# Loading and computing the opening of a hybrid layer by halves of the features

## The chip, the core and the metric

One core of a Trainium2 chip runs the whole layer in one launch. The metric is the device time of the launch in microseconds; lower is better. Five engines work side by side and meet only at semaphores: TensorE (PE, matmuls), VectorE (DVE), ScalarE (ACT), GpSimd (POOL) and SyncE (SP, which issues most of the DMAs). ScalarE and GpSimd issue DMAs too, in the order of their own instructions.

## The reference, cut to what matters

384 tokens (128 of context, 256 latent) of 1024 features go through a layer. At its start stand the modulation (a silu of a conditioning vector times `w_ada`, 12 chunks of 512 columns here: shift is chunks 0 and 1, scale chunks 2 and 3) and the first projection `w_in`:

```python
mod = (silu(c) @ w_ada + b_ada).reshape(1, N_MOD, D_MODEL)       # one for the context, one for the latents
h = rmsnorm(x, g_pre_mix) * (1.0 + scale_a) + shift_a
z = h @ w_in            # u, q, k, v, o (512 columns each) and 16 gate columns
y = concat(pool_mixer(u), bidirectional_mlstm(q, k, v, o, gates)) @ w_out
x = x + gate_a * rmsnorm(y, g_post_mix)
x = x + gate_f * rmsnorm(moe(rmsnorm(x, g_pre_ffn) * (1 + scale_f) + shift_f), g_post_ffn)
```

`moe` routes each token to 6 of 64 experts (1024 to 2 x 256 to 1024). Chunks 0 and 2 of `w_ada` are the first 512 features of shift and scale, chunks 1 and 3 the last 512. In z the features are summed over, so the first 512 features of h and of `w_in`'s rows give half of every sum.

## The kernel before, in words

**Weights.** The 20 weight chunks of 2 MB of the opening (a0 to a11 of `w_ada`, q, k, v, o, u of `w_in`, w0 and w1 of `w_out`, s) go through four slots `w_gu`, chunk number i of the list `order` (L444) in slot i mod 4. SyncE issues their loads in order (L629 to 641; o before a7), q in two halves of four feature blocks (L635 with semaphore `q_in`, L636). Before a chunk that reuses a slot it waits until the slot's last chunk was used (`gu_used`).

**Modulation.** `ada(i)` (L1685) multiplies a chunk of `w_ada` into bank 6 or 7 on TensorE for i under 4; `ada_evac` (L1055) adds the bias into `modrow`, `one_plus` (L1068) makes (1 + scale) times the gain, four small matmuls (L1728) turn the rows into columns in bank 6, and a copy (L1078) puts them into `modT`. For i from 4 to 9 VectorE makes the products itself (`ada_sums`, L1101, L1125 and L1130), in banks 4 and 5 for a4, 6 and 7 for the others.

**Tokens.** The normalised tokens are transposed into banks 0 to 5 (L1723). `shifted` applies scale and shift to a block of 128 features, blocks 0 to 3 on VectorE (L1083) and 4 to 7 on ScalarE (L748). Products are made with an fp32 operand split in two parts: `high` (L731, L740) and `high_tokens` (L751, L756) on ScalarE make the rounded parts `w_hi` and `tT_hi`, `low` (L518, L524) on GpSimd and `low_tokens` (L1086, L1089) on VectorE the rests `w_lo` and `tT_lo`. `PARTS` lists the feature blocks that one `high_tokens` takes. Each product is three matmuls (`three`, L529 to 531).

**Products.** `z_chunk` (L1733) runs over the two halves of the features of q, k, v, o, u, and in a half over the four (or three) units of the chunk, each in a bank of its own (`z_bank`). q comes first, then the gates' products in bank 0, then k, which waits until VectorE is done with a4 (banks 4 and 5). There are two buffers `w_hi`; the next chunk's half waits until the half before last is used.

**ScalarE's order.** After the last `high_tokens` ScalarE issues seven DMAs (L769 to 777: `poolm`, `w_pool`, state_C, `pool_scale`, state_n, the router's weights and bias), and only then comes `high(2)`, the first half of k. Rows of 4 bytes: `pool_scale` has 512 of them, state_n 1024; `w_pool` and state_C have 512 + 1024 rows of 512 bytes.

Of the kernel before, what the change touches and what calls it, by code (L numbers as in the profile page):

```python
# [14 lines left out]
P = 128  # L15
D = 1024
NC = D // P
T_CTX, T_LAT = 128, 256
T = T_CTX + T_LAT
# [84 lines left out]
ALU = mybir.AluOpType  # L104
# [70 lines left out]
def build_layer(nc, t_in, t_out):  # L175
    with ExitStack() as ctx:
# [254 lines left out]
        def row_from_dram(engine, dst, m, first, semaphore):  # L431
# [11 lines left out]
        COL = {"u": 0, "q": MW, "k": 2 * MW, "v": 3 * MW, "o": 4 * MW}  # L443
        order = ["a0", "a1", "a2", "a3", "q", "a4", "a5", "k", "v", "a6", "a7", "o", "u", "a8", "a9",  # L444
                 "w0", "w1", "a10", "a11", "s"]
# [48 lines left out]
        def z_bank(n):  # L494

            w, i = z_units[n]
            return (1, 2, 6, 7)[i] if w == "q" else 2 + i

# [7 lines left out]

        PARTS = ((0, 2), (2, 4), (4, 8))

# [115 lines left out]
        def _(sp):  # L624
            for i in range(NT):
                src = t_in["x_prompt"][0] if i == 0 else t_in["x_sample"][0, P * (i - 1):P * i, :]
                sp.dma_start(x[:, i, :], src).then_inc(x_in, 16)
            a7, o = chunk["a7"], chunk["o"]
            for name in order[:a7] + ["o", "a7"] + order[o + 1:]:  # L629
                i = chunk[name]  # L630
                s = i % PSLOTS
                if i >= PSLOTS:
                    sp.wait_ge(gu_used[s], i // PSLOTS)
                if name == "q":
                    sp.dma_start(w_gu[s][:, 0:NC // 2, :], chunk_source(name)[:, 0:NC // 2, :]).then_inc(q_in, 16)  # L635
# [81 lines left out]
        def _(a):  # L717
# [33 lines left out]
            def high_tokens(first, end):  # L751
                if first < 4:
                    a.wait_ge(h1_dve, 2 * end)
                else:
                    a.wait_ge(h1_act, NC)
                a.activation(tT_hi[first // 4][:, first % 4:end - 4 * (first // 4), :], hT[:, first:end, :], ACT.Copy)\  # L756
                    .then_inc(th_ready, 1)

            a.wait_ge(modT_ready, 1)
            shifted(4)  # L760
            shifted(5)
            high_tokens(*PARTS[0])
            shifted(6)
            high_tokens(*PARTS[1])
            high(1)
            shifted(7)
            high_tokens(*PARTS[2])

            a.dma_start(poolm[:, :, :].rearrange("p g n -> p (g n)"), t_in["pool_constants"]).then_inc(pool_in, 16)  # L769
# [38 lines left out]
            a.wait_ge(mod_a_ready, 1)  # L808
            for m in range(2):
# [224 lines left out]
        def _(v):  # L1034
# [38 lines left out]
            for i in (0, 2, 1, 3):  # L1073
                ada_evac(i)
            v.wait_ge(mod_ready, 4)
            one_plus(2, 0).then_inc(mod_a_ready, 1)
            v.wait_ge(modT_done, 1)
            v.tensor_copy(modT[:, :, :, :].rearrange("p a c m -> p (a c m)"), bank(6, P, P + 32)).then_inc(modT_ready, 1)  # L1078
            v.wait_ge(modT_ready, 1)

            def shifted(c):
                for m, (lo, hi) in enumerate(((0, T_CTX), (T_CTX, T))):
                    v.tensor_scalar(hT[:, c, lo:hi], psum[:, T * c + lo:T * c + hi], modT[:, 1, c, m:m + 1],  # L1083
                                    modT[:, 0, c, m:m + 1], ALU.mult, ALU.add).then_inc(h1_dve, 1)
# [7 lines left out]

            shifted(0)
            shifted(1)
            shifted(2)
            low_tokens(0)
            shifted(3)
            low_tokens(1)
            low_tokens(2)

            def ada_sums(i, c_first=0, c_end=NC):  # L1101

                n = chunk[f"a{i}"]
                s = n % PSLOTS
                done = 15 * sorted(ada_acc).index(i)
                if c_first == 0:
                    v.wait_ge(gu_in[s], 16 * (n // PSLOTS + 1))
                    if i >= 6:
                        wait_chunk(v, f"a{i - 1}")
                    if i == 4:  # L1110
                        v.wait_ge(h1_act, NC)
# [29 lines left out]
            ada_sums(4)  # L1141
            ada_sums(5, 0, 3)

            v.wait_ge(gates_done, 1)
            for b, dst in enumerate((g_in, g_lf)):
                own.add(v.tensor_scalar(dst[0:32, :], bank(0, 0, T)[64 * b:64 * b + 32, :], b_gate[0:32, b:b + 1], None, ALU.add))
                for tile in range(NT):
                    ins = v.tensor_scalar(dst[32:36, P * tile:P * tile + P],
                                          bank(0, 0, T)[64 * b + 32:64 * b + 36, natural(1, tile)],
                                          b_gate[32:36, b:b + 1], None, ALU.add)  # L1150
                    own.add(ins)
# [15 lines left out]
            v.tensor_tensor(g_b[:, :], g_b[:, :], g_mx[:, :], ALU.add).then_inc(scans_ready, 1)  # L1167
            ada_sums(5, 3)
            v.wait_ge(scans_ready, 1)
# [463 lines left out]
        def _(g):  # L1633
# [18 lines left out]

            for k in range(12):
                low(g, k)
# [29 lines left out]
        def _(t):  # L1684
# [32 lines left out]
            ada(0)  # L1717
            ada(1)
            t.wait_ge(const_in, 16)
# [4 lines left out]
            ada(2)  # L1724
            ada(3)
            t.wait_ge(mod_a_ready, 1)
            for i in range(4):
                ins = t.matmul(bank(6, P + 8 * i, P + 8 * i + 8), modrow[:, i, :],  # L1728
                               ident.rearrange("p (j r) -> p j r", j=4)[:, :, 0:2], start=True, stop=True)
            ins.then_inc(modT_done, 1)  # L1730


            def z_chunk(w):  # L1733
# [3 lines left out]
                for half in range(2):  # L1737
                    t.wait_ge(w_lo_ready, SPLIT.index((w, half)) + 1)
                    if w == "q":
                        t.wait_ge(tl_ready, 1 if half == 0 else len(PARTS))  # L1740
                    for n in units:
                        i = z_units[n][1]
                        prior = before(n)
                        if half == 0 and prior is not None:
# [4 lines left out]
                        for j in range(4):  # L1749
                            c = 4 * half + j  # L1750
                            if n == 0 and c == PARTS[1][0]:
                                t.wait_ge(tl_ready, 2)
                            if w in "qk":
# [12 lines left out]
            for w in "qkvou":  # L1766
# [454 lines left out]
```

## Time and profile before

| | us |
|---|---|
| three runs | 761.12, 762.65, 764.17 |
| median | 762.65 |
| the profiled execution | 762.65 |
| its span in the trace | 760.6 |
| TensorE busy | 700.4 (92%) |
| VectorE busy | 404.3 (53%) |
| ScalarE busy | 190.5 (25%) |
| GpSimd busy | 84.7 (11%) |
| HBM read | 254.64 MB, 340 GB/s over the span |

The span runs from the first to the last instruction of the trace; 2.05 us lie around it. The layer's stages in the trace: the opening up to 42 us, the projections up to about 141 us, the mixers and `w_out` up to about 209 us, then the router and the experts, whose weight loads start at 214.5 us. Busy time is a sum over stages with different limits, so each step is read from the rows of its own stage. Durations in the rows are those of one execution.

### The profile page before, as it was taken

The page shows a single profiled execution, that of the slowest core. Times are in us where ns is not written, and L with a number is a line of the kernel's source. Part 1 is how long each engine was busy: PE and PEld are TensorE (multiplying, and loading weights), DVE is VectorE, ACT ScalarE, POOL GpSimd, SP SyncE. Part 2 cuts the span into 40 slices and gives each one's busy share as a digit, 9 for nine tenths or more (in the row PEclk, how much of TensorE's full clock was granted, in tenths as well). Part 3 has the DMA queues.
Part 4 walks back from the last instruction along what each step waited for, and adds up shares of the span by engine and source line. Part 5 has one row for each costly group of instructions (what it writes and reads, how often), then busy time and mean ns, then how long its engine had stood idle before and what let it go on. Part 6 is the DMA issues. An engine that isn't in the chain of part 4 may idle for free.

```text
span 760.6 us, 11595 instructions
## 1 busy us (share of the span) xinstructions
PE 700.4 (92%) x4241; PEld 403.9 (53%) x4241; DVE 404.3 (53%) x1004; ACT 190.5 (25%) x320; POOL 84.7 (11%) x49
## 2 busy tenths in 40 slices
PE   1679999899989999999999999999999999989785
PEld 1579888688866645544444444444444445433232
DVE  3078999477085754454544545454454464434234
ACT  3145422474264112212111111211211111111003
POOL 2244444411400100000000000000000000000000
PEclk9879999999999999999999999999999999999999
DMA  9998576623669559879999999999999999999982
GB/s 325 382 379 260 181 258 225 248 86 94 211 247 422 245 209 399 332 320 382 421 419 421 423 421 419 421 420 420 420 420 421 420 421 421 421 422 418 421 343 92
DMA packets 56766, 259.17 MB, mean 341 GB/s; under 512 B 7296, under 2 KB 9952, under 8 KB 31488
## 3 DMA queue, kind: packets, MB, share of 16 engines
q1 hardware_dynamic: 48720, 249.05, 81.5%
q0 software_dynamic: 1808, 5.92, 2.3%
q10 hardware_dynamic: 6176, 3.40, 1.5%
q8 instruction: 36, 0.59, 0.3%
q14 instruction: 26, 0.21, 0.1%
HBM read 254.64 MB, written 3.71 MB: 340 GB/s over the span
## 4 chain that ended last, share of the span: by engine, by line
PE 65%; DMA 14%; DVE 12%; SPq 5%; ACT 2%; issue 1%; ACTq 0%; DVEq 0%
PE psum L2056 19%; DMA w_gu<-in_w_expert_gu 11%; PE psum L2068 10%; PE psum L1949 9%; PE psum L2027 7%; PE psum L529 4%; PE psum L531 4%; PE psum L530 4%; DVE psum L1130 3%; DMA w_gu<-in_w_ada 3%; PE psum L1930 3%; DVE f_acc L1537 2%; SPq L665 2%; SPq L674 2%; PE psum L1961 1%
## 5 line engine op out<-in xcount | busy, mean ns | idle before, releaser
L2056 PE MATMUL psum<-w_gu,hgT 128*32 128x512 f32 (+1 forms) x1280 | 192.1, 594 | 10.3 <-DMA w_gu<-in_w_expert_gu 10.3
L2056 PEld LDWEIGHTS psum<-w_gu,hgT 128*32 128x32 f32 (+1 forms) x1280 | 58.1, 119 | 136.6 <-issue 136.4
L1537 DVE TENSOR_TENSOR f_acc<-f_acc,psum 128x512 f32<-128x512 f32 x156 | 106.1, 687 | 45.5 <-PE psum L2027 42.3
L2068 PE MATMUL psum<-w_dn,actT 128*32 128x512 f32 (+1 forms) x640 | 98.5, 596 | 0.5 <-ACT actT L951 0.5
L1522 DVE SCALAR_TENSOR_TENSOR act<-sil,wsl,psum 128x256 f32<-128x256 f32 x27 | 18.3, 680 | 135.4 <-ACT sil L976 127.1
L2027 PE MATMUL psum<-y_hi,onehotT 128*128 128x512 f32 x156 | 67.7, 434 | 4.5 <-DVE f_acc L1537 2.5
L524 POOL TENSOR_TENSOR w_lo<-w_gu,w_hi 128x2048 fp32r<-128x2048 f32 x14 | 64.3, 4599 | 62.9 <-ACT w_hi L740 62.9
L1949 PE MATMUL psum<-onehot,h_hi 128*128 128x512 f32 (+1 forms) x168 | 67.3, 401 | 0.0
L1949 PE MATMUL psum<-onehot,h_lo 128*128 128x512 f32 (+1 forms) x168 | 64.9, 386 | 0.0
L1528 DVE TENSOR_TENSOR y_lo<-psum,y_hi 128x1024 fp32r<-128x1024 f32 x27 | 33.0, 1224 | 54.2 <-ACT y_hi L980 54.2
L2027 PE MATMUL psum<-y_lo,onehotT 128*128 128x512 f32 x156 | 61.3, 393 | 0.0
L980 ACT ACTIVATE y_hi<-psum 128x1024 fp32r<-128x1024 f32 x27 | 27.6, 1024 | 122.0 <-PE psum L2068 122.0
L2068 PEld LDWEIGHTS psum<-w_dn,actT 128*32 128x32 f32 (+1 forms) x640 | 27.0, 119 | 57.6 <-issue 56.8
L976 ACT ACTIVATE sil<-psum 128x256 f32<-128x256 f32 x27 | 10.4, 384 | 183.6 <-PE psum L2056 183.6
L432 POOL DMA_DIRECT2D gate_ctx<-mod_rows x1 | 0.6, 586 | 483.0 <-DVE act L1522 483.0
L971 ACT ACTIVATE hgT<-psum 128x512 f32<-128x512 f32 (+1 forms) x56 | 32.6, 582 | 80.9 <-PE psum L1949 80.9
L1130 DVE SCALAR_TENSOR_TENSOR psum<-w_gu,scT,psum 128x512 f32<-128x512 f32 x72 | 48.2, 750 | 0.0
L529 PE MATMUL psum<-w_hi,tT_hi 128*128 128x512 f32 x120 | 47.3, 394 | 0.0
L531 PE MATMUL psum<-w_hi,tT_lo 128*128 128x512 f32 x120 | 46.7, 390 | 0.0
L530 PE MATMUL psum<-w_lo,tT_hi 128*128 128x512 f32 x120 | 46.7, 389 | 0.0
L740 ACT ACTIVATE w_hi<-w_gu 128x2048 fp32r<-128x2048 f32 x14 | 26.8, 1914 | 72.1 <-PE psum L531 28.2
L1949 PEld LDWEIGHTS psum<-onehot,h_hi 128*128 128x128 f32 x168 | 31.5, 187 | 23.5 <-issue 18.1
(293 smaller groups left out, 864.0 us busy)
## 6 DMA issues: line engine op xcount, KB each, us to landing
w_gu<-in_w_expert_gu SPq DMA_DIRECT2D x128, 1024.0 KB, 19.8
w_dn<-in_w_expert_down SPq DMA_DIRECT2D x64, 1024.0 KB, 18.8
w_gu<-in_w_ada SPq DMA_DIRECT2D x12, 2048.0 KB, 15.9
w_gu<-in_w_in SPq DMA_DIRECT2D x4, 2048.0 KB, 8.7
w_gu<-in_w_out SPq DMA_DIRECT2D x2, 2048.0 KB, 10.4
bc<-mod_rows POOLq DMA_DIRECT2D x6, 512.0 KB, 7.3
w_gu<-in_w_in SPq DMA_DIRECT2D x2, 1024.0 KB, 15.8
w_gu<-in_w_shared_gu SPq DMA_DIRECT2D x1, 2048.0 KB, 9.3
```

The costliest lines, as they stand in the source:

```text
L524: engine.tensor_tensor(w_lo[s][:, cs, :], w_gu[s][:, cs, :], w_hi[half][:, :, :].bitcast(F32), ALU.subtract)\
L529: t.matmul(out, lhs[0], rhs[0], start=start, stop=False)
L530: t.matmul(out, lhs[0], rhs[1], start=False, stop=False)
L531: return t.matmul(out, lhs[1], rhs[0], start=False, stop=stop)
L971: a.activation(dst, src, ACT.Copy).then_inc(hgT_ready, 1)
L1130: ins = v.scalar_tensor_tensor(out, w, k, part, ALU.mult, ALU.add)
L1528: v.tensor_tensor(y_lo[:, :], bank(3, 0, 1024), y_hi[:, :].bitcast(F32), ALU.subtract).then_inc(y_ready, 1)
L1537: v.tensor_tensor(dst, dst, bank(5 + n), ALU.add).then_inc(f_added, 1)
L1949: ins = t.matmul(bank(c % 2, 0, width), part[:, i, c, :], onehot[b % 2][:, i, 0:width], start=(n == 0), stop=(n == 2 * NT - 1))
L2027: ins = t.matmul(bank(5 + n), onehotT[par][:, i, :], part[:, 512 * n:512 * (n + 1)], start=(part is y_hi), stop=(part is y_lo))
L2056: ins = t.matmul(bank(2)[rows, :], column(c)[:, rows], w_gu[s][:, c, :], start=(c == 0), stop=(c == NC - 1), tile_position=(0, rows.start))
L2068: ins = t.matmul(bank(3 + n)[rows, :], actT[:, j, rows], w_dn[s][:, j, 512 * n:512 * (n + 1)], start=(j == 0), stop=(j == 1), tile_positio ...
```

## The change

The opening is done in two halves of the features. SyncE loads a0, a2 and the first half of q, then a1, a3, the second half of q, a4, k, v, and a5 only behind v. The modulation is made per half (`modulation(half)`, `modulation_T(half)`), so that `mod_a_ready` and `modT_ready` count to 2. Blocks 3 and 7 are shifted on ScalarE, the other six on VectorE; `PARTS` has four entries of two blocks. On TensorE the transposes stand in front of ada(2), ada(1) behind the first half's modulation, ada(3) in front of q's third unit and the second half's modulation in front of q's fourth. q's third unit is in bank 0, the gates' products in bank 6, and a5's sums are no longer begun before the gates' evacuation. GpSimd makes the first `w_lo` before it issues its small loads.

```diff
-        order = ["a0", "a1", "a2", "a3", "q", "a4", "a5", "k", "v", "a6", "a7", "o", "u", "a8", "a9",
+        order = ["a0", "a2", "q", "a1", "a3", "a4", "a5", "k", "v", "a6", "a7", "o", "u", "a8", "a9",
...
-            return (1, 2, 6, 7)[i] if w == "q" else 2 + i
+            return (1, 2, 0, 7)[i] if w == "q" else 2 + i
...
-        PARTS = ((0, 2), (2, 4), (4, 8))
+        PARTS = ((0, 2), (2, 4), (4, 6), (6, 8))
+        ON_ACT = (3, 7)
...
-            for name in order[:a7] + ["o", "a7"] + order[o + 1:]:
+            issued = ["a0", "a2", "q", "a1", "a3", "q", "a4", "k", "v", "a5", "a6", "o", "a7"] + order[chunk["u"]:]
+            for turn, name in enumerate(issued):
...
             a.wait_ge(modT_ready, 1)
-            shifted(4)
-            shifted(5)
+            shifted(3)
             high_tokens(*PARTS[0])
-            shifted(6)
             high_tokens(*PARTS[1])
             high(1)
+            a.wait_ge(modT_ready, 2)
             shifted(7)
             high_tokens(*PARTS[2])
+            high_tokens(*PARTS[3])
...
+            def modulation(half):
+
+                ada_evac(half)
+                ada_evac(2 + half)
+                v.wait_ge(mod_ready, 2 * half + 2)
+                v.scalar_tensor_tensor(modrow[:, 2 + half, :], modrow[:, 2 + half, :], 1.0, grow[:, 0, half, :],
+                                       ALU.add, ALU.mult).then_inc(mod_a_ready, 1)
+                v.wait_ge(modT_done, half + 1)
+                v.tensor_copy(modT[:, :, 4 * half:4 * half + 4, :],
...
-            shifted(0)
-            shifted(1)
-            shifted(2)
-            low_tokens(0)
-            shifted(3)
-            low_tokens(1)
-            low_tokens(2)
+            for half in range(2):
+                modulation(half)
+                for c in range(4 * half, 4 * half + 3):
+                    shifted(c)
+                low_tokens(2 * half)
+                low_tokens(2 * half + 1)
...
             ada_sums(4)
-            ada_sums(5, 0, 3)
...
-            ada_sums(5, 3)
+            ada_sums(5)
...
+            low(g, 0)
             g.wait_ge(gu_in[3], 16)
             g.dma_start(wgs[:, :, :], w_in[:, :, 5 * MW:5 * MW + 16]).then_inc(gate_in, 16)
...
             ada(0)
-            ada(1)
...
             ada(2)
-            ada(3)
...
+            modulation_T(0)
+            ada(1)
...
+                        if (w, half, i) == ("q", 0, 2):
+                            ada(3)
+                        if (w, half, i) == ("q", 0, 3):
+                            modulation_T(1)
...
-                        ins = three(t, bank(0, 0, T), (wg_hi[:, c, :], wg_lo[:, c, :]),
+                        ins = three(t, bank(6, 0, T), (wg_hi[:, c, :], wg_lo[:, c, :]),
```

## Rows read from the trace of the kernel before

**Rows 1.** Busy time in one stretch; columns: us, five engines, clock, DMA share, GB/s.
```profile
300.00:700.00 400.00, 392.90 (x2338) 181.09 (x2336) 191.75 (x503) 67.55 (x114) 0.00 (x0) 1.00 0.99 409
```

**Rows 2.** Chain of waits in order of time; columns: start, us, what.
```profile
10.80 21.52 DMA w_gu<-in_w_ada
```

**Rows 3.** Timeline of the opening; columns: start, us, engine, line, operation, idle before, releaser.
```profile
15.35 3.64 PE L1697 MATMUL psum<-w_gu,scT 128*32 128x128 f32 x64 [15.35 <-DMA w_gu<-in_w_ada]
...
23.82 2.84 PE L1723 MATMUL psum<-const,xn 128*128 128x128 f32 x24
...
26.95 1.95 PE L1697 MATMUL psum<-w_gu,scT 128*32 128x128 f32 x64 [0.29 <-DMA w_gu<-in_w_ada]
...
32.37 2.57 PE L1697 MATMUL psum<-w_gu,scT 128*32 128x128 f32 x64 [3.46 <-DMA w_gu<-in_w_ada]
...
35.02 1.91 ACT L740 ACTIVATE w_hi<-w_gu 128x2048 fp32r<-128x2048 f32 x1 [22.28 <-DMA w_gu<-in_w_in]
...
35.50 0.42 DVE L1070 SCALAR_TENSOR_TENSOR modrow<-modrow,grow 128x256 f32<-128x256 f32 x1
...
35.98 1.88 PE L1728 MATMUL psum<-const,modrow 128*128 128x8 f32 x8 [1.05 <-DVE modrow L1070]
37.01 4.50 POOL L524 TENSOR_TENSOR w_lo<-w_gu,w_hi 128x2048 fp32r<-128x2048 f32 x1 [1.15 <-ACT w_hi L740]
...
38.12 2.40 DVE L1083 TENSOR_SCALAR hT<-psum,modT 128x128 f32<-128x128 f32 x6
...
40.66 1.67 DVE L1089 TENSOR_TENSOR tT_lo<-hT,tT_hi 128x768 fp32r<-128x768 f32 x1
...
42.48 0.66 PE L529 MATMUL psum<-tT_hi,w_hi 128*128 128x384 f32 x1 [4.62 <-DVE tT_lo L1089]
```

**Rows 4.** Timeline from the gates' products to u, one engine after the other.
```profile
61.75 0.34 PE L529 MATMUL psum<-tT_hi,wg_hi 128*128 128x384 f32 x1
...
66.68 0.41 PE L529 MATMUL psum<-tT_hi,w_hi 128*128 128x384 f32 x1 [0.52 <-issue]
...
64.01 1.40 DVE L1125 TENSOR_SCALAR psum<-w_gu,scT 128x512 f32<-128x512 f32 x2
...
101.46 0.69 DVE L1179 COPY v<-psum 128x512 f32<-128x512 f32 x1 [0.34 <-PE psum L531]
...
138.30 1.91 ACT L740 ACTIVATE w_hi<-w_gu 128x2048 fp32r<-128x2048 f32 x1 [3.50 <-PE psum L531]
```

**Rows 5.** ScalarE's queue in the timeline; then DMA issues: KB each, us to landing.
```profile
48.03 6.29 ACTq L773 DMA_DIRECT2D small<-in_pool_scale  x1
...
55.80 3.54 ACTq L776 DMA_DIRECT2D w_router<-in_w_router  x1
...
59.93 1.92 ACT L740 ACTIVATE w_hi<-w_gu 128x2048 fp32r<-128x2048 f32 x1 [11.83 <-issue]
...
c0n<-in_state_C ACTq DMA_DIRECT2D x1, 512.0 KB, 11.9
...
w_gu<-in_w_in SPq DMA_DIRECT2D x1, 2048.0 KB, 23.9
```

**Rows 6.** Timeline: a VectorE instruction beside one of GpSimd.
```profile
77.39 4.78 DVE L1165 TENSOR_SCALAR g_lf<-g_mx 36x384 f32<-36x384 f32 x1
...
77.33 4.62 POOL L524 TENSOR_TENSOR w_lo<-w_gu,w_hi 128x2048 fp32r<-128x2048 f32 x1 [6.20 <-ACT w_hi L740]
```

**Rows 7.** DMA queues at 53 to 54, then 54 to 55: packets, MB, share.
```profile
q10 hardware_dynamic: 32, 0.33, 78.8%
q1 hardware_dynamic: 32, 0.07, 16.9%
...
q1 hardware_dynamic: 146, 0.30, 78.5%
q10 hardware_dynamic: 133, 0.06, 21.2%
```

**Rows 8.** Busy time and clock, the columns of rows 1.
```profile
46.00:47.00 1.00, 1.00 (x5) 1.00 (x4) 0.00 (x0) 0.97 (x3) 1.00 (x1) 0.50 1.06 391
```

More of the change, by code:

```diff
@@ L627, in _ @@
                 sp.dma_start(x[:, i, :], src).then_inc(x_in, 16)
-            a7, o = chunk["a7"], chunk["o"]
-            for name in order[:a7] + ["o", "a7"] + order[o + 1:]:
+            issued = ["a0", "a2", "q", "a1", "a3", "q", "a4", "k", "v", "a5", "a6", "o", "a7"] + order[chunk["u"]:]
+            for turn, name in enumerate(issued):
                 i = chunk[name]
@@ L633, in _ @@
                     sp.wait_ge(gu_used[s], i // PSLOTS)
+                if name == "q" and "q" in issued[turn + 1:]:
+                    sp.dma_start(w_gu[s][:, 0:NC // 2, :], chunk_source(name)[:, 0:NC // 2, :]).then_inc(q_in, 16)
+                    continue
                 if name == "q":
-                    sp.dma_start(w_gu[s][:, 0:NC // 2, :], chunk_source(name)[:, 0:NC // 2, :]).then_inc(q_in, 16)
                     sp.dma_start(w_gu[s][:, NC // 2:NC, :], chunk_source(name)[:, NC // 2:NC, :]).then_inc(gu_in[s], 16)
@@ L751, in high_tokens @@
             def high_tokens(first, end):
[L752 to L755, printed above, removed]
+                here = [c for c in range(end) if c in ON_ACT]
+                a.wait_ge(h1_dve, 2 * (end - len(here)))
+                if here:
+                    a.wait_ge(h1_act, 2 * len(here))
                 a.activation(tT_hi[first // 4][:, first % 4:end - 4 * (first // 4), :], hT[:, first:end, :], ACT.Copy)\
@@ L807, in _ @@
                             g_b[32 * d:32 * d + H, T_CTX - 1:T_CTX]).then_inc(m_out, 16)
-            a.wait_ge(mod_a_ready, 1)
+            a.wait_ge(mod_a_ready, 2)
             for m in range(2):
@@ L1071, in one_plus @@
                                               ALU.add, ALU.mult)
[L1073 to L1079, printed above, removed]
+            def modulation(half):
[6 more added lines that the diff above has]
+                v.tensor_copy(modT[:, :, 4 * half:4 * half + 4, :],
+                              bank(6, P, P + 32).rearrange("p (a c m) -> p a c m", a=2, c=NC)[:, :, 4 * half:4 * half + 4, :])\
+                    .then_inc(modT_ready, 1)
+                v.wait_ge(modT_ready, half + 1)
             def shifted(c):
+                if c + 1 in ON_ACT:
+                    v.wait_ge(h1_act, 2 * ON_ACT.index(c + 1) + 2)
                 for m, (lo, hi) in enumerate(((0, T_CTX), (T_CTX, T))):
@@ L1110, in ada_sums @@
                     if i == 4:
-                        v.wait_ge(h1_act, NC)
+                        v.wait_ge(h1_act, 2 * len(ON_ACT))
                     elif i == 5:
@@ L1141, in _ @@
             ada_sums(4)
-            ada_sums(5, 0, 3)
             v.wait_ge(gates_done, 1)
             for b, dst in enumerate((g_in, g_lf)):
-                own.add(v.tensor_scalar(dst[0:32, :], bank(0, 0, T)[64 * b:64 * b + 32, :], b_gate[0:32, b:b + 1], None, ALU.add))
+                own.add(v.tensor_scalar(dst[0:32, :], bank(6, 0, T)[64 * b:64 * b + 32, :], b_gate[0:32, b:b + 1], None, ALU.add))
                 for tile in range(NT):
                     ins = v.tensor_scalar(dst[32:36, P * tile:P * tile + P],
-                                          bank(0, 0, T)[64 * b + 32:64 * b + 36, natural(1, tile)],
+                                          bank(6, 0, T)[64 * b + 32:64 * b + 36, natural(1, tile)],
                                           b_gate[32:36, b:b + 1], None, ALU.add)
@@ L1650, in _ @@
                         .then_inc(gate_in, 16)
-            for k in range(12):
+            for k in range(1, 12):
                 low(g, k)
@@ L1724, in _, with modulation_T @@
             ada(2)
-            ada(3)
[L1726 to L1730, printed above, removed]
+            def modulation_T(half):
+                t.wait_ge(mod_a_ready, half + 1)
+                if half:
+                    t.wait_ge(modT_ready, half)
+                for i in (half, 2 + half):
+                    ins = t.matmul(bank(6, P + 8 * i, P + 8 * i + 8), modrow[:, i, :],
+                                   ident.rearrange("p (j r) -> p j r", j=4)[:, :, 0:2], start=True, stop=True)
+                ins.then_inc(modT_done, 1)
+            modulation_T(0)
+            ada(1)
             def z_chunk(w):
@@ L1739, in z_chunk @@
                     if w == "q":
-                        t.wait_ge(tl_ready, 1 if half == 0 else len(PARTS))
+                        t.wait_ge(tl_ready, 2 * half + 1)
                     for n in units:
                         i = z_units[n][1]
+                        if (w, half, i) == ("q", 0, 2):
+                            ada(3)
+                        if (w, half, i) == ("q", 0, 3):
+                            modulation_T(1)
                         prior = before(n)
@@ L1750, in z_chunk @@
                             c = 4 * half + j
-                            if n == 0 and c == PARTS[1][0]:
-                                t.wait_ge(tl_ready, 2)
+                            if n == 0 and j == 2:
+                                t.wait_ge(tl_ready, 2 * half + 2)
                             if w in "qk":
```

## The prediction, made before the changed kernel was run

> **What bounds the kernel now.** I read four views, in this order. First the page and the windows. From 300 us on the DMA engines are busy 0.99 of the time at 409 GB/s and TensorE 392.9 of 400 us [rows 1]: the expert stage is full on both, its loads start only when the slots of the opening come free, so what the opening gains or loses moves the end by as much. Second the chain of waits of the opening: loads of `w_gu` up to 32.37, then a serial stretch (ada(3), the transposes of the modulation, shift and scale, tokens' parts) until the first product of q at 42.48 [rows 2, 3]. Third TensorE: q's products 42.48 to 61.75, the gates' to about 66.2, k's from 66.68, and from there its only idle time of note is 0.7 us until u is done at 138.3, where `high(11)`, which waits for it, starts [rows 3, 4]. VectorE runs beside it: v's last copy at 101.46 waited 0.34 us for TensorE, and from there VectorE is full up to `u_tok` at 141.36 [rows 4]. So TensorE and VectorE meet at 101.46 with 0.34 us between them, and a shift of TensorE's chain from k on is a shift of the end. Fourth, what lets k start: not q. ScalarE issues seven DMAs from 46.62 to 59.83, can make `w_hi` of k only at 59.93 (k landed at 34.97 + 23.9 = 58.9), GpSimd needs 4.6 us more for `w_lo`, and k starts at 66.68, 0.5 us after the gates' products [rows 5]. **The start of k is set twice over**, by TensorE's own work (66.2) and by ScalarE's queue (66.6). A change of the first alone gives nothing.
>
> **The loads.** Bytes on SP's queue up to a load fix its landing, as the engines are full: 3.67 MB at 15.35, 7.87 at 26.95, 9.97 at 32.37, 11.0 (first half of q) at 35.02 [rows 3]. By these points the new order lands a0 at 15.35, a2 about 21, half of q 23.8, a1 29.6, a3 35.0, the rest of q 37.7 to 38.3 (GpSimd's small loads dip the rate), a4 43, k 48.5. The bytes ahead of k's end shrink by one chunk; v takes the place of a5, which now waits until q is used.
>
> **First half.** TensorE: ada(0) 15.35 to 18.99, transposes (2.84, up to 5 at half rate) to 22.3, ada(2) 1.95 to 24.3; evacuations 0.49, `one_plus` half of 0.42, four small matmuls half of 1.88, copy 0.19 [rows 3]: modT's first half at 26.2 instead of 38.08. VectorE's six shifts 2.40 to 28.65, parts of the tokens about 0.85 each. `w_hi` 23.8 to 25.7 and `w_lo` to 30.3; the first `low_tokens` has two SBUF inputs, and one such row ended 0.8 us after GpSimd's w_lo did (42.33 against 41.51) [rows 3], so 31.2 and 32.1. ada(1) at 29.6 takes 2.5 to 3.6 us: 32.1 to 33.3. Then q's first two units, 24 matmuls; warm ones start 0.175 us apart (from 61.58, with the gates' first at 61.75 [rows 4]), 4.2 us: 37.2. **q starts about 9.7 us earlier** (32.8 against 42.48).
>
> **Second half.** ada(3) 37.2 to 39.2; evacuation 39.8; `one_plus` 0.3; unit 2 of q 39.2 to 41.3; modulation_T(1) 41.8; copy 42.1; shifts to 44.5; `low_tokens` 45.5 and 46.4; unit 3 runs beside them. q's second half, 48 matmuls x 0.174 = 8.3, to 54; gates 4.4 (61.75 to 66.15), to 58.4. That is 7.8 us before 66.2. Moved work: a4's sums run 46.4 + 1.3 (casts) + 10.7 (they ended at 64.01, where a5's start) = 58.4 [rows 4], in time for k, which waits for them. The first three channels of a5's sums (4.0 us: 1.40 + 2.6, 64.01 to 67.94 [rows 4]) now lie behind the gates, in VectorE's way; in exchange VectorE starts 5.5 us earlier, and L1165, which stood 4.4 us behind GpSimd (4.78 for 384 columns, GpSimd's w_lo ran 77.33 to 81.95 [rows 6]), falls elsewhere. VectorE reaches a5's end near 88 against 89.57: it is not the bound, and is priced at nothing; if its cover went it would cost up to 4 us. The bank changes (q's unit 2, the gates) cost nothing: bank 0 is free after the shifts, bank 6 after the copy of modT. GpSimd's five small issues (some 3 us) now follow its first `w_lo`, 30.3 to 33.6, and land some 6 us later, before the casts at 46.4. The new waits: VectorE's third shift of a half waits for ScalarE's two (0.86 us, side by side); TensorE's modulation_T(1) stands in front of q's unit 3 alone, and that unit is back before `low_tokens` of the second half is ready, so its wait is covered; without that cover it would cost 0.8 us.
>
> **ScalarE's queue: where the gain goes.** Its seven issues stand behind the last `high_tokens`, which starts at 44.6 instead of 46.62. Their 13.2 us are waiting, not issuing: L773 took 6.29 and ended at 54.32, as `poolm`'s last packets went [rows 7], L776 took 3.54 and ended at 59.34, as state_C landed (47.47 + 11.9) [rows 5]. How fast they drain depends on what SP's queue has in flight. While `poolm` moved, SP's queue (q1) and ScalarE's (q10) got 32 packets each in one us; in the next, 146 of q1 (0.30 MB) stood against 133 of q10 (0.06 MB), 78.5% of the time against 21.2% [rows 7]: **one packet in turn, 2 KB against 0.5 KB**. Before, q1 ran dry behind k, since v waited until q was used (61.75). After, `poolm` moves 48.5 to 52.5; q1 then holds about 41 packets per engine of k and v (behind `poolm` about 19 were left before; the start is 1.9 us earlier, at the 12 per us of 0.39 MB), and **a5 adds 64 from 55.2**, a6 64 from 59.5, since a4 is done sooner. w_pool and state_C have (512 + 1024)/16 = 96 packets per engine, a pair costs 0.785 x 16/146 + 0.212 x 16/133 = 0.086 + 0.026 = 0.112 us. The unknown is how much of it must be gone before L776 ends. Lower bound 56 packets (state_n's 64 and w_router's 8 per engine then find the room that was left when L773 ended): 52.9 + 56 x 0.112 + the slowest engine's 0.8 = 60.0, and one more us for the issues: free at 61.2, k at 61.2 + 1.92 + 4.6 + 0.1 = 67.8. Upper bound for these two: all 96, free at 63.8, k at 70.5. I take 69.0, +2.3 against 66.68; the row nearest to it (L776 ended with state_C's landing) is for the later end. Below nothing: were the 13.2 us a fixed length, k would start 1.9 to 2.1 earlier.
>
> **The clock.** TensorE would stand idle from 58.4 to 69. After 4.6 us of idling at 37.9 its granted clock read 0.50 (1.2 GHz) until 47.1, 0.50 still at 46 to 47 [rows 8]: 4.6 us at half rate, 2.3 lost. Taken: 2.1; bounds 0 (short gap) and 2.3.
>
> **Sum.** The profiled execution took 762.65 with a span of 760.6, and 762.65 is also the median of the three runs. +2.3 (start of k) + 2.1 (clock) + 0 (VectorE) = +4.4: **767.0**, slower by 0.6%.
>
> **A rule against a row.** The `one_plus` of the second half starts at 39.8, and GpSimd's `w_lo` of q's second half at 39.7 to 40.3. Beside GpSimd the rows show waiting of TENSOR_TENSOR [rows 3] and TENSOR_SCALAR [rows 6], none of SCALAR_TENSOR_TENSOR with both inputs in SBUF. The Trainium skill (SBUF — State Buffer, Who interferes with whom) says that a VectorE instruction with two SBUF inputs contends with a GpSimd one that reads SBUF, and that the one issued first blocks the other; by it `one_plus` would wait too. No row here shows that form. If it waits, it waits out GpSimd's 4.5 us.
>
> **Rivals.**
> Not slower: `one_plus` comes second and waits to 44.3. Then shifts end at 47.8, q ends at 57.4 to 59, gates at 61.6 to 63.6, ScalarE issues from 47.9. `poolm` is through at 55.8, q1 has about 3 packets per engine left and a5 comes only at 58.5 or later, when the 96 small ones are nearly gone: 3 x 0.112 + 93 x 0.027 = 2.9 us, 58.7 to 60.3. k starts at 66.5 to 67.5, after a gap of 3 to 5 us (clock 0 to 2): +0 to +3, 764. It decides from a `one_plus` that starts after GpSimd. For it: the two are 0.5 us apart. Against: in the new order the landing that starts GpSimd is the one that slips. Chance 0.27.
> Worse: L776 needs state_n's 4-byte packets gone too, 96 more per engine, each in turn with a 2 KB packet of a5 and a6: 0.099 x 60 to 80 = 6 to 8 us more, k at 76: +9.5 + 2.1, 774. For: in the quarter microseconds to 59.3 most of them had gone. Against: L774 itself took only 1.42. Chance 0.17.
> Faster: the seven issues keep their length, or q10 is not held by a5; k at 64.6, gap 6 us: -2.1 + 0 to 2, about 761.5; were k free to start at the gates' end, 58.9 for 66.7, 754.9. For: VectorE, TensorE and k's landing (about 50) would all allow it. Against: ScalarE's 11.83 us before `high` [rows 5]. Chance 0.20, most of it on gains above 4 us that some looser queue would bring.
> That the change does not do what it says (q not earlier): only if ada(1) or the first shift were late by 10 us; under 0.02, within the others.
>
> **How the numbers follow.** Forecast 0.36 (765.5 to 769), not slower 0.27 (762 to 766), worse 0.17 (771 to 776), faster 0.20 (754 to 762). The range for 8 in 10: 757 to 774. About 0.5% (3.8 us) is what a measurement of this kernel can tell from no change. Slower by more: 0.27 of the forecast + 0.17 + 0.03 = 0.47; within: 0.09 + 0.22 + 0.06 = 0.37; faster: 0.14 + 0.02 = 0.16.
>
> **What would show it.** First product of q at 32 to 34; `one_plus` of the second half short (0.3) or over 4 us; q's end at 54 or 57 to 59; ScalarE's issues from 44.6 or 47.9 and their length (13.2, 17, 25 us); a gap of TensorE before k and the granted clock behind it; q1 and q10 with equal packets at 55 to 62; every later stage shifted by k's amount. The prediction is wrong if ScalarE's `high` of k starts before 58, or if the chain from k on is no longer rigid.

## The result and the profile after

| | us | ratio to before, 95% interval |
|---|---|---|
| kernel before, 15 runs | 762.63 (761.12 to 764.4) | |
| changed kernel, 15 runs beside them | 765.4 (763.6 to 767.46) | 1.0034 [1.0022, 1.0047] |
| changed kernel again, 8 runs, beside 19 of before (762.46) | 766.51 (764.17 to 768.02) | 1.005 [1.0033, 1.0068] |
| the profiled executions: before, after | 762.65, 765.4 (spans 760.6, 763.3) | |

The change makes the kernel slower by 0.3 to 0.5%. The forecast was 767.0 with a range of 757 to 774. On the first set the whole interval lies inside 0.5%, a case that had been given 0.37 against 0.47 for slower by more; the second set straddles that bound. Further down each ratio is to runs of the kernel before on the same chip (their medians: 761.76, 762.46 and 762.2), so the ratios can be compared with each other, the times only roughly.

The opening did what it was meant to do. The timeline of the changed kernel, opening (start, us, engine, line, operation, idle time before and its releaser); it answers to [rows 3]:

```profile
15.42 3.40 PE L1706 MATMUL psum<-w_gu,scT 128*32 128x128 f32 x64 [15.42 <-DMA w_gu<-in_w_ada]
...
23.43 1.91 ACT L743 ACTIVATE w_hi<-w_gu 128x2048 fp32r<-128x2048 f32 x1 [10.66 <-DMA w_gu<-in_w_in]
...
25.43 4.52 POOL L525 TENSOR_TENSOR w_lo<-w_gu,w_hi 128x2048 fp32r<-128x2048 f32 x1 [16.56 <-ACT w_hi L743]
...
27.89 3.74 DVE L1099 TENSOR_TENSOR tT_lo<-hT,tT_hi 128x768 fp32r<-128x768 f32 x2
29.23 3.33 PE L1706 MATMUL psum<-w_gu,scT 128*32 128x128 f32 x64 [4.13 <-DMA w_gu<-in_w_ada]
...
32.49 0.45 PE L530 MATMUL psum<-tT_hi,w_hi 128*128 128x384 f32 x1
...
39.40 0.29 DVE L1081 SCALAR_TENSOR_TENSOR modrow<-modrow,grow 128x128 f32<-128x128 f32 x1
...
40.34 4.57 POOL L525 TENSOR_TENSOR w_lo<-w_gu,w_hi 128x2048 fp32r<-128x2048 f32 x1 [7.18 <-ACT w_hi L743]
...
45.87 0.66 PE L530 MATMUL psum<-tT_hi,w_hi 128*128 128x384 f32 x1 [2.20 <-DVE tT_lo L1099]
```

q's first product starts at 32.49, ten microseconds before the 42.48 of [rows 3]. Its second half starts at 45.87, after 2.20 us of idling.

The same timeline from there to k and v, and at the first expert load; it answers to [rows 4, 5]:

```profile
44.15 0.33 ACTq L772 DMA_DIRECT2D poolm<-in_pool_constants  x1
...
45.56 7.77 ACTq L776 DMA_DIRECT2D small<-in_pool_scale  x1
...
53.36 2.42 ACTq L777 DMA_DIRECT2D c0n<-in_state_n  x1
55.80 3.58 ACTq L779 DMA_DIRECT2D w_router<-in_w_router  x1
59.41 0.50 ACTq L780 DMA_DIRECT2D b_router<-in_b_router  x1
60.01 1.91 ACT L743 ACTIVATE w_hi<-w_gu 128x2048 fp32r<-128x2048 f32 x1 [15.03 <-issue]
...
62.00 9.35 POOL L525 TENSOR_TENSOR w_lo<-w_gu,w_hi 128x2048 fp32r<-128x2048 f32 x2 [17.10 <-ACT w_hi L743]
63.33 3.58 DVE L1161 SCALAR_TENSOR_TENSOR g_t<-g_lf 36x384 f32<-36x384 f32 x1
...
66.61 0.66 PE L530 MATMUL psum<-tT_hi,w_hi 128*128 128x384 f32 x1 [6.42 <-POOL w_lo L525]
...
102.82 0.69 DVE L1187 COPY v<-psum 128x512 f32<-128x512 f32 x1 [0.35 <-PE psum L532]
...
217.38 2.77 SPq L655 DMA_DIRECT2D w_gu<-in_w_expert_gu  x2
```

The gates' products end at 60.2 instead of 66.2. ScalarE makes `w_hi` of k at 60.01, as before (59.93, [rows 5]): its issues began 2.5 us earlier (44.15 for 46.62) and were held 2.6 us longer (15.8 us for 13.2). k starts at 66.61, as before (66.68, [rows 4]), and TensorE has idled for 6.42 us. The six microseconds won at the gates are all lost in front of k.

Then k costs more. Busy time and clock of the changed kernel in four stretches (us, five engines, clock, DMA share, GB/s), and of the kernel before in the last two of them:

```profile
45.00:49.00 4.00, 3.13 (x10) 3.16 (x11) 3.86 (x12) 0.00 (x0) 0.00 (x0) 0.59 1.10 418
62.00:70.00 8.00, 3.39 (x12) 3.42 (x13) 7.93 (x6) 6.85 (x9) 8.00 (x2) 0.57 1.05 383
142.00:147.00 5.00, 4.14 (x24) 3.32 (x28) 0.91 (x3) 1.62 (x4) 4.18 (x1) 1.00 1.04 398
158.00:166.00 8.00, 8.00 (x38) 7.32 (x37) 4.64 (x18) 4.42 (x16) 0.00 (x0) 0.57 0.01 3
```

```profile
142.00:147.00 5.00, 5.00 (x18) 3.81 (x16) 0.00 (x0) 1.56 (x3) 2.81 (x1) 0.66 1.05 396
158.00:166.00 8.00, 8.00 (x61) 7.13 (x61) 7.11 (x25) 5.62 (x22) 0.00 (x0) 1.00 0.00 0
```

TensorE's granted clock is at half (1.2 GHz) for part of q's second half and again around the start of k. So v's last copy comes 36.21 us behind k's start instead of 34.78: 102.82 against 101.46, +1.36. From there to the first expert load 114.56 us pass for 113.03. In this stretch before has one low spell of about 3 us, at 143 to 146, and after one of about 7 us, at 158 to 165; +1.53. From the load to the end of the span it is 545.92 against 546.11, -0.19. The sum, +2.70, is the difference of the spans. So only +1.36 lies in the stretch that the change touches. The +1.53 comes with the length and the place of a low spell; the second execution of the changed kernel, below, has a shorter spell there and no such loss.

### The profile page after: what moved, and what is told of

It is laid out like the page before. It is cut to its first block, busy times and chain, and to the rows that moved or that the text cites. A ratio compares the mean times of both kernels' runs of the same rounds, so it can differ in the third digit from the quotient of the medians.

```text
span 763.3 us, 11603 instructions
## 1 busy us (share of the span) xinstructions
PE 702.9 (92%) x4241; PEld 405.9 (53%) x4241; DVE 410.7 (54%) x1011; ACT 189.4 (25%) x317; POOL 84.8 (11%) x49
## 4 chain that ended last, share of the span: by engine, by line
PE 64%; DMA 13%; DVE 11%; SPq 5%; ACT 2%; ACTq 2%; issue 1%; POOL 1%; DVEq 0%
PE psum L2074 19%; DMA w_gu<-in_w_expert_gu 11%; PE psum L2086 10%; PE psum L1967 9%; PE psum L2045 7%; DVE psum L1139 3%; PE psum L530 3%; PE psum L532 3%; PE psum L531 3%; PE psum L1948 3%; DMA w_gu<-in_w_ada 2%; DVE f_acc L1545 2%; SPq L668 2%; SPq L677 2%; PE psum L1979 1%
```

## The experiments

### Is it ScalarE's queue that holds k?

The four issues that wait longest are moved behind v's parts, in the changed kernel and, to see what they are worth alone, in the kernel before.

```diff
@@ ScalarE, behind the last high_tokens
             a.dma_start(poolm, ...); a.dma_start(w_pool, ...); a.dma_start(c0n, state_C ...)
-            a.dma_start(pool_scale, ...)
-            a.dma_start(c0n, state_n ...)
-            a.dma_start(w_router, ...)
-            a.dma_start(b_router, ...)
@@ ScalarE, behind high(5), in front of the g_post_ffn issues
+            (the same four)
```

> The changed kernel with ScalarE's last four issues (pool_scale, state_n, the router's two) moved from in front of high(2) to behind high(5); the three large ones stay. Theory (ScalarE's queue holds k): high(2) starts as soon as k has landed and q's first half is used, about 50 to 53 us instead of 60.0; w_lo of k is ready before 60; k starts at 60.2, straight behind the gates' products, instead of 66.61, and its granted clock stays 1.00. Time 765.4 - 6.4 - 1.4 = 757.6, up to 760 if one of VectorE's scans falls behind GpSimd's w_lo. Rival (k held by its landing, or by VectorE's a4 sums at 58.6): k starts at 60 to 63. Rival (VectorE's chain is the bound after all): k starts at 60.2, but v's last copy moves by under 3 us and the time is 763 or more.

Measured: **755.3 us**, ratio 0.9921 [0.9894, 0.9948]. Timeline of this kernel:

```profile
49.16 1.92 ACT L743 ACTIVATE w_hi<-w_gu 128x2048 fp32r<-128x2048 f32 x1 [3.36 <-DMA w_gu<-in_w_in]
...
57.28 1.59 DVE L1139 SCALAR_TENSOR_TENSOR ada_acc<-w_gu,scT,psum 128x512 f32<-128x512 f32 x2
...
58.93 0.44 PE L530 MATMUL psum<-tT_hi,w_hi 128*128 128x384 f32 x1
...
93.78 0.69 DVE L1187 COPY v<-psum 128x512 f32<-128x512 f32 x1 [0.34 <-PE psum L532]
```

> The kernel before with the same four issues moved behind high(5). Theory (the start of k is set twice over, by TensorE at 66.15 and by ScalarE's queue at 66.55): high(2) starts when k has landed and q's first half is used, before 59 us, but k starts at 66.2 instead of 66.68: gain 0.5 us, 762.1, no change. Rival (ScalarE's queue alone holds the projections, also in the kernel before): a gain of 3 us or more.

Measured: 763.15 us, ratio 1.0002 [0.9988, 1.0017]. Timeline:

```profile
58.52 1.92 ACT L740 ACTIVATE w_hi<-w_gu 128x2048 fp32r<-128x2048 f32 x1 [10.77 <-DMA w_gu<-in_w_in]
```

With the queue out of the way, `w_hi` of k waits only for k's own load, k follows the gates without idling at 58.93, and v's last copy comes 7.68 us earlier than before. Of these 6.16 are left at the first expert load (208.33 for 214.49), since this execution too has a low spell of 7 us there, at 149 to 156. The experiment's own expectation was 757.6 and k at 60.2; k came 1.3 us sooner, because the clock stayed at 1.00 in q's second half. The forecast had named just this case: k at 58.9 and 754.9 us, against a measured 755.3, or 756.6 by the ratio. What holds k next is close: VectorE's last sums of a4 end at 58.87. The same edit alone gives no change that can be measured, since k's load lands only at 58.5 there and q and the gates last as long: its first product of k is at 65.69. So the start of k was set more than once, and neither half of the pair, the halves in the opening or the later issues, gains anything without the other. Together they beat both kernels.

Once more on another chip:

> The changed kernel with the four issues moved behind high(5), once more on another chip. Theory (the opening by halves is worth what the start of k may move, once ScalarE is free and k's columns are landed at 49 us): 755 to 757.5 us, 0.7 to 1.0% under the kernel before; k starts at 58.5 to 59.5. Rival (the first interval was luck of the clock's patches): 760 or more.

Measured: 756.74 us, ratio 0.9928 [0.9902, 0.9954]; k starts at 59.26, v's last copy at 94.09.

### What holds ScalarE's queue?

Either the issues take what they take, or the transfers on SP's queue decide it. First SP's queue is emptied: v and all behind it are held until `w_hi` of k is made.

```diff
             for turn, name in enumerate(issued):
+                if name == "v":
+                    sp.wait_ge(w_hi_ready, 3)
```

> The changed kernel with the load of v (and so a5 and all behind it) held until high(2) is done. Theory (the two queues take turns packet by packet, so q1's backlog stretches q10's drain): behind poolm (51.5) only little of k is in flight, the 96 packets of 512 bytes per engine take 2.6 us instead of 6 and the 4-byte ones 1.4; ScalarE is free at 56 to 57 instead of 60.0, k starts at 62.8 to 63.5, the time is 761 to 763. Rival (the issues have a length of their own, about 13 to 15 us whatever else is in flight): ScalarE free at 57.5 to 60 and k at 64 to 66.6. Rival (v then lands too late for its high at about 75): a gap of TensorE before v.

Measured: 759.2 us, ratio 0.9968 [0.9947, 0.999]. Timeline:

```profile
46.02 3.54 ACTq L778 DMA_DIRECT2D small<-in_pool_scale  x1
...
54.89 1.92 ACT L745 ACTIVATE w_hi<-w_gu 128x2048 fp32r<-128x2048 f32 x1 [9.44 <-issue]
...
61.60 0.41 PE L530 MATMUL psum<-tT_hi,w_hi 128*128 128x384 f32 x1 [1.28 <-issue]
```

The `pool_scale` issue takes 3.54 us where it took 7.77, the seven together 10.2 for 15.8. Nothing on ScalarE was touched. I had expected ScalarE free at 56 to 57 and 761 to 763 us; it was free at 54.9, and the time by the ratio is 760.2. k starts 5.0 us earlier than in the changed kernel, v's last copy only 3.9 (98.9 for 102.82):

```profile
97.66 1.88 DVE L1189 COPY v<-psum 128x512 f32<-128x512 f32 x3
```

The three copies stand in a row with no wait for TensorE. Here VectorE, busy with its own sums until then, is the bound.

Then SP's queue is made longer, by a copy of 2 MB from HBM to HBM in 2 KB rows behind v.

```diff
+        spare = nc.dram_tensor("spare", [P, NC, MW], F32).ap()
@@ SyncE, after v's load
+                if name == "v":
+                    sp.dma_start(spare, chunk_source("o")).then_inc(spare_in, 16)
```

> The changed kernel with one more transfer of 2 MB in rows of 2 KB (a copy in HBM that nobody reads) on SP's queue behind v. Theory (q10 moves one packet for each of q1's while q1 has any, and ScalarE is free only when the small packets are nearly gone): between 51.5 and 60 q1 and q10 move equal numbers of packets, ScalarE's seven issues end 4 to 8 us later than at 59.9, k starts at 71 to 75, the time is 769 to 775. Rival (the issues have a length of their own): they end at 60 and the time stays at 765 to 766.

Measured (four runs): 770.79 us, ratio 1.0109 [1.0086, 1.0133]. Timeline, and the DMA queues of this kernel from 66 to 67 us (packets, MB, share of the 16 engines' time):

```profile
61.07 3.54 ACTq L785 DMA_DIRECT2D b_router<-in_b_router  x1
...
71.29 0.66 PE L532 MATMUL psum<-tT_hi,w_hi 128*128 128x384 f32 x1 [10.71 <-POOL w_lo L527]
```

```profile
q1 hardware_dynamic: 181, 0.37, 96.4%
q10 hardware_dynamic: 181, 0.00, 10.2%
```

ScalarE's queue (q10) carries rows of 4 bytes here, 181 packets and not 0.01 MB, against as many 2 KB packets of SP's (q1). This is after ScalarE was free (64.6); while it was held, the numbers were as equal, with rows of 512 bytes in q10: 156 against 156 from 57 to 58. ScalarE's seven issues are the same in three kernels and took 10.2 us with v held, 15.8 in the changed kernel and 20 here: what differs is the neighbour. The Trainium skill (DMA: Bandwidth & Descriptors, Queues, rings and completion order) says that a DMA engine goes round the queues that have work, a packet from each; the trace agrees, with 181 against 181. (The profile's packets are single rows here; whether a turn takes one row or several, the equal counts don't tell.)

The changed kernel, run again, shows the same thing by itself.

> The changed kernel itself, on the same chip as f1 to f3. Every theory: 1.0034 times the kernel before; the granted clock is low at 63 to 70 behind the gap before k.

Measured: 766.51 us, as in the table above. Timeline of its profiled execution, its clock from 61 to 74, and its DMA queues from 60 to 61:

```profile
59.20 2.88 ACTq L780 DMA_DIRECT2D b_router<-in_b_router  x1
62.18 1.91 ACT L743 ACTIVATE w_hi<-w_gu 128x2048 fp32r<-128x2048 f32 x1 [16.44 <-issue]
...
68.78 0.66 PE L530 MATMUL psum<-tT_hi,w_hi 128*128 128x384 f32 x1 [9.84 <-POOL w_lo L525]
...
106.19 0.69 DVE L1187 COPY v<-psum 128x512 f32<-128x512 f32 x1 [0.35 <-PE psum L532]
```

```profile
61.00:74.00 13.00, 5.22 (x16) 5.26 (x17) 4.62 (x9) 8.84 (x10) 9.04 (x2) 0.50 0.85 283
```

```profile
q1 hardware_dynamic: 168, 0.34, 96.1%
q10 hardware_dynamic: 170, 0.01, 13.5%
```

The kernel is the same; what differs is TensorE's clock in q's second half. It stayed at 1.00 from 46 to 49, so q was used, and a5 issued, at 54.72 instead of 55.97. a5's packets then met the last 4-byte rows, the last issue took 2.88 us instead of 0.50, and k started at 68.78 instead of 66.61. **In this pair the earlier q is done, the later k starts.** In the other execution most of the small rows were through before a5's stood beside them; its DMA queues from 58 to 59:

```profile
q10 hardware_dynamic: 1232, 0.12, 100.4%
q1 hardware_dynamic: 45, 0.09, 33.6%
```

It is not a rule for every microsecond. In the variants with 26, 18 and 32 extra matmuls, below, a5 was issued at 56.28, 56.43 and 57.84, and `w_hi` of k started at 60.50, 59.96 and 60.22, as with 55.97 (60.01). Only the one execution with 54.72 has 62.18, so the late form is seen once. ScalarE's issues also began later there, at 44.90 for 44.15; with 26 extra they began at 44.74 and `w_hi` came at 60.50, so this alone does not seem to explain the 2 us.

To take a5 alone out of the way, it and what follows are held, v is not.

```diff
             for turn, name in enumerate(issued):
+                if name == "a5":
+                    sp.wait_ge(w_hi_ready, 3)
```

> The changed kernel with v's load in its place, and only a5 and what follows it on SP's queue held back until ScalarE's high(2) is done. Theory (a5's packets, brought forward with q, share the turns with the 4-byte rows and delay ScalarE's release): the 4-byte rows have only v beside them, so ScalarE is free at 59 to 60 us whatever TensorE's clock does in q's second half, high(2) at about 59.9, k starts at 66.5 to 66.7; v's last copy 101.5 to 102.9; time 764 to 765.5, that is 0 to 1.5 us under the changed kernel. Rival (v's packets alone set ScalarE's release and a5 adds nothing): no difference to the changed kernel's profile, in both of its forms (k at 66.6 or at 68.8). If k lies above 68 here, the theory is wrong.

Measured: 764.55 us, ratio 1.0025 [1.001, 1.004]. Timeline:

```profile
59.99 1.91 ACT L745 ACTIVATE w_hi<-w_gu 128x2048 fp32r<-128x2048 f32 x1 [14.62 <-issue]
...
66.58 0.66 PE L530 MATMUL psum<-tT_hi,w_hi 128*128 128x384 f32 x1 [6.33 <-POOL w_lo L525]
```

These are the numbers expected, but the profiled execution had the low clock in q's second half (0.73 at 46 to 48, 0.50 to 50), so that a5 would have come late anyway: its `w_hi` alone can't tell the theory from the rival. The median is about 1 us under the changed kernel's first set, with intervals that overlap. What stands is that ScalarE is held to 60 us with v alone in its way. That a5, where it comes early, adds the rest is read from the packets of the second execution, and not shown by this run.

### What does k's idle start cost?

Extra matmuls of a full tile, into a bank nobody reads, stand between the gates' products and k: 32, 18 and 26 of them.

```diff
@@ TensorE, in front of k's first half
+                    for u in range(32):
+                        t.matmul(bank(3, 0, T), wg_hi[:, u % NC, :], tT_hi[0][:, u % 4, :], start=True, stop=True)
```

> The changed kernel with 32 further matmuls of 384 columns between the gates' products and k; their result is overwritten and read by nobody. They take 5.6 us of the 6.4 us in which TensorE stands idle. Theory (what the change costs is the clock behind that gap): k starts at 66.6 as in the changed kernel, the granted clock stays 1.00 from 63 to 70, v's last copy comes 1.4 us earlier, the time is 763.3 (1.4 to 2.5 less than 765.4), the same as before. Rival (the loss has another cause, a later stage or VectorE's own work): the clock stays up and the time stays at 765.

Measured: 763.94 us, ratio 1.0031 [1.0008, 1.0054]. Timeline and clock:

```profile
61.89 5.81 PE L1795 MATMUL psum<-tT_hi,wg_hi 128*128 128x384 f32 x32
67.54 0.33 PE L530 MATMUL psum<-tT_hi,w_hi 128*128 128x384 f32 x1
```

```profile
66.00:70.00 4.00, 4.00 (x25) 4.00 (x24) 4.00 (x2) 3.10 (x4) 4.00 (x2) 1.00 1.01 382
```

> The changed kernel with 18 further matmuls (3.1 us) between the gates' products and k, instead of the 32 of e3, which overran the gap when the clock was low in q's second half (k at 67.5). Theory (the clock behind the gap is the cost): k starts at 66.6, the clock is 1.00 from 66 to 70 or falls later than in the changed kernel, the time is 1 to 2.5 below the changed kernel on the same chip (f4). Rival (other cause): no difference to f4.

Measured: 766.4 us, ratio 1.0049 [1.0031, 1.0068], no difference to the changed kernel on that chip (1.005). k started at 66.60, after 2.78 us without a matmul, and the clock was 0.50 at 67 to 70.

> The changed kernel with 26 extra matmuls of a full tile between the gates and k, so that TensorE is busy in the 6.4 us gap. Theory (k's stage is 1.4 us dearer because it begins on an idle, low-clocked TensorE): the granted clock is 1.00 behind the start of k, v's last copy follows k's start by 34.8 us instead of 36.2, k starts at 66.6 to 67.0 and the time is 764.0 to 764.6. Rival (the fall of the clock has another cause than the gap): the clock falls to 0.50 behind k's start all the same, 36 us from k to v's last copy, and the time is 765.4 or more.

Measured: 764.21 us, ratio 1.0019 [0.9998, 1.0039]. Timeline and clock:

```profile
63.68 1.40 PE L1795 MATMUL psum<-tT_hi,wg_hi 128*128 128x384 f32 x7
67.17 0.42 PE L530 MATMUL psum<-tT_hi,w_hi 128*128 128x384 f32 x1 [2.09 <-issue]
```

```profile
67.00:71.00 4.00, 3.83 (x13) 3.86 (x14) 4.00 (x2) 2.37 (x4) 4.00 (x2) 0.57 1.03 379
```

The 32 filled the whole gap and 0.9 us more; the clock stayed full, and 34.71 us passed from k's start to v's last copy. The other two sets left 2.8 and 2.1 us, and the clock fell behind the start of k as in the changed kernel. So these two did not keep the clock, and can't say what it costs. With 26, 764.21 lies where I had expected it, but the clock fell and 36.37 us passed, as the rival had it: that number was luck. Nor does the launch time show the price: with 32, 1.0031 against the changed kernel's 1.0034, where 1.4 to 2.5 us less had been expected; 0.9 us of that went into k's later start. The times differ by less than their intervals. What the clock costs up to v's last copy is read from this table of the profiled executions (the version with v held is left out, as TensorE isn't the bound there):

| kernel | k starts | idle before | v's last copy | between |
|---|---|---|---|---|
| before | 66.68 | 0.52 | 101.46 | 34.78 |
| changed, later issues | 58.93 | none | 93.78 | 34.85 |
| changed, 32 extra | 67.54 | none | 102.25 | 34.71 |
| changed | 66.61 | 6.42 | 102.82 | 36.21 |
| changed, 18 extra | 66.60 | 2.78 | 102.95 | 36.35 |
| changed, 26 extra | 67.17 | 2.09 | 103.54 | 36.37 |
| changed, a5 held | 66.58 | 6.33 | 103.30 | 36.72 |
| changed, again | 68.78 | 9.84 | 106.19 | 37.41 |
| changed, more traffic | 71.29 | 10.71 | 108.71 | 37.42 |

Without idling, or after 0.52 us of it, it is 34.7 to 34.9 us (three executions more, of the version with later issues and of before with later issues, have 34.7 to 34.8); with a low clock at the start, 1.4 to 2.7 us more.

### Is q's second half on the path of the faster version?

In the version with later issues, 12 extra matmuls bridge the gap between q's halves.

```diff
@@ TensorE, in front of q's second half
+                    t.wait_ge(modT_ready, 2)
+                    for u in range(12):
+                        ins = t.matmul(bank(6, 0, T), w_hi[0][:, u % 4, 0:DH], tT_hi[0][:, u % 4, :], start=True, stop=True)
```

> The kernel of e1_after_late (four issues behind high(5)) with 12 further matmuls of 384 columns between q's two halves, where TensorE stands idle for about 2 us; their result is read by nobody. Theory (the gates' end now sets k's start, and a granted clock of 0.50 in q's second half moves it): the clock stays 1.00 from 44 to 50 in every execution, k starts at 58.6 to 58.9, the time is 754 to 755.5, 0 to 1.5 below e1. Rival (TensorE's own work there is covered by VectorE's sums of a4, at 58.6): no difference to e1.

Measured (six runs): 756.87 us, ratio 0.994 [0.9916, 0.9963]; v's last copy at 93.72 (93.78 without). No gain: there the clock was at 1.00 in q's second half without the extra matmuls too, in both traces, so there was nothing to give back. The rival, that VectorE's sums of a4 hold k anyway, stays open; they end 0.06 us before k starts.

## Where the prediction was right and where not

**The opening: right.** First product of q at 32.8, came 32.49. The stall of the first `low_tokens` behind GpSimd came (3.74 us for two, against 2.34 for the two of the second half), and so did ada(1) at 29.6 (29.23) and ada(3) at 37.2 (36.85). a4's sums ended at 58.6 (forecast 58.4).

**q's end: half right.** 54 was forecast, and a5 in flight from 55.2. a5 was issued at 54.72 in one execution and at 55.97 in the other, where the clock fell at q's second half. I had looked at the clock in front of k only; the gap of about 2 us between q's halves follows from the forecast's own numbers (unit 2 to 41.3, so unit 3 to about 43.5; `low_tokens` at 45.5), but I did not draw it, nor ask for its price.

**VectorE: right.** It is not the bound. v's last copy still waits 0.32 to 0.36 us for TensorE in every kernel but the one with v held.

**The start of k: the turns right, the route and in one of two executions the size off.** The step was "+2.3 against 66.68". It came -0.07 (66.61) and +2.10 (68.78). Turns, packet for packet against 2 KB ones, are what the emptied and the lengthened queue show: k at 61.60 and 71.29. What I had taken for settled was that a5 comes in time to collide. With q done 1.25 us later it didn't.

Where it did, +2.10 for +2.3 is in part luck. The sum let a5 stand beside the 512-byte rows from 55.2 on. In fact SP's queue had nearly run dry between 57 and 58 in both executions (48 and 40 packets), and nearly all of the 512-byte rows were through by 59. What a5 met were the 4-byte rows: from 60 to 61 in the second execution 157 of q10's 170 packets were under 512 bytes. That is the mechanism of the *worse* rival, in a smaller size. The sum's bounds don't match each other either: the lower adds 0.8 and 1 us to the drain, the upper doesn't; by the lower one's recipe the upper is k at about 72.

**The clock: right in kind, +2.1 forecast, +1.43 and +2.63 measured** (36.21 and 37.41 less 34.78). The second lies above the bound of 2.3. That bound rests on a row read only from 37.9 on: in the kernel before, the clock had fallen at about 33.6 already (0.78 at 33 to 34, 0.50 from 34 to 47), so the 4.6 us of idling at 37.9 were not what brought it down. The price goes with how long the clock stays low behind k's start: 3.0 us in the first execution (to 69.6), 5.7 in the second (to 74.5). In the second execution start and clock together are +4.73 at v's last copy; the sum of the forecast was +4.4.

**The sum.** Forecast +4.4; measured +2.75 and +3.6 in the profiled executions, +2.8 and +4.05 by the medians. In the first, k's start is the missing term, and of the +2.75 only +1.36 comes by the way that was forecast; +1.53 is the spell in a later stage, which the forecast did not have. That the total lies so near is luck. In the second the +4.73 at v's last copy is there, but 1.4 us came back before the expert loads. I see nothing of the change in that, for the same changed kernel has it both ways: the stretch from v's last copy to the first expert load takes 111.3 us in three executions of variants (a5 held, 26 and 32 extra), 111.6 in two (again, more traffic), 113.03 in that of before, and 114.5 to 114.6 in six: the changed kernel's first, the one with 18 extra matmuls, the three of the version with later issues, and before with later issues. The three at 111.3 have no low spell in that stage, the two at 111.6 and before have one of about 3 us, and the six long ones all have one of about 7 us between 149 and 166; before, with later issues, has it too, without a change in that stage. All four traces with later issues are long ones; whether that is chance is open. How often each kind comes in unprofiled runs I can't tell, and so not how much of the medians' difference it is. It isn't small: of the eleven runs of the first set with later issues, the five with a mean clock of 0.991 took 753.3 to 754.8 us, the others 755.3 to 761.8.

**The rivals.** *Not slower* rested on a second `one_plus` that comes behind GpSimd. It didn't: `one_plus` took 0.29 at 39.40, GpSimd began at 40.34. That the time came near its 764 has another reason, the late a5. But the form that had no row does wait: the SCALAR_TENSOR_TENSOR of the gates (L1161) took 3.58 us beside `w_lo`, and the same instruction took 0.55 before, as GpSimd's `w_lo` ended (77.33 less 6.20 of idling is 71.13, [rows 6], and it started at 71.05). It ended at 66.91, and the `w_lo` beside it at about 66.7 (62.00 and half of 9.35). The Trainium skill (SBUF — State Buffer, Who interferes with whom) had said so of two SBUF inputs; the trace agrees, with 3.58. *Worse* rested on 4-byte rows that take turns with 2 KB ones. They do (170 against 168, 181 against 181), but a5 meets only the last of them, and it costs 2.2 us, not 6 to 8. *Faster*, with k at 58.9, was the right reading of what the rest of the kernel allows; it wanted an edit that the change lacks.

## What to carry to other kernels

When a stage's start is set twice over, take both away or neither: an earlier opening without the queue gave +0.3 to +0.5%, the queue without the opening nothing, both -0.7 to -0.8%. Small-row DMAs that ScalarE had to issue before its next piece of work made it wait for what the neighbouring queue carried (10.2 to 20 us for the same seven), so try them behind the work and not ahead of it. And a gap of 2 to 11 us in front of TensorE's work wasn't free: up to v's last copy it cost 1.4 to 2.7 us here on top of its own length.

## What the runs showed of the hardware that I had not expected

Two hardware queues that both have work got equal numbers of packets even where one has 4 bytes in its packet: 181 against 181 in one microsecond, 10.2% of the engines' time for the one and 96.4% for the other.

The same kernel has two forms, 1.25 us apart at q's end. In its two profiled executions the granted clock in q's second half was once 0.50 and once 1.00, after idling for 2.20 and 1.68 us, and a5's issue, ScalarE's release and k's start differ with it.

Low spells of the clock also stand in stretches in which TensorE is busy throughout (158 to 166, busy 8.00 of 8.00). But each stands behind a gap. In the mixers' stage the clock fell 1.3 to 2.3 us after TensorE had taken up work again, and what lay before was 0.7 to 2.1 us of idling; in the changed kernel it fell at 158.4, behind 1.32 us that ended at 156.63. So it was in ten of the thirteen traces; the other three have the same gaps and no spell. A long spell goes with 3.2 us more in that stage (114.55 for 111.34), which is more than the whole effect that was measured here. So a pair of profiled executions is read stretch by stretch, and not by its end.
